# Ordering the experts of a mixture by their row counts on the chip, and moving a list behind the first expert

## The reference

```
logits = xt @ w_router + b_router              # 1024 tokens, 32 experts
top_vals, top_idx = top_k(logits, 4)
gates = softmax(top_vals)
xs = xt[tok]                                   # 4096 rows, sorted by expert
h = ragged_dot(xs, w_gate_up, group_sizes) + b_gate_up[e]
act = min(glu, 7) * sigmoid(1.702 * glu) * (clip(lin, -7, 7) + 1)
y = ragged_dot(act, w_down, group_sizes) + b_down[e]
out = segment_sum(y * gate, tok)
```

## Time and profile before

| | us |
|---|---|
| median of 3 runs | 3243.78 |
| lowest and highest | 3241.05, 3246.48 |
| the profiled execution | 3245.3 |
| its span, first to last instruction | 3243.0 |
| TensorE busy in it | 2861.4 (88%) |
| VectorE, ScalarE, GpSimd busy | 1193.4, 612.3, 196.7 |
| mean granted TensorE clock | 0.944 of full speed |

### The profile page before, as it was taken

One profiled execution on the slowest core, in us unless ns is written; L12 is line 12 of the kernel. 1 busy time (PEld: TensorE's weight loads), 2 busy tenths in 40 slices (PEclk: granted clock), 3 DMA queues, 4 the chain that ended last, 5 costly groups with the idle time before them and its releaser, 6 DMA issues.

```text
span 3243.0 us, 53552 instructions
## 1 busy us (share of the span) xinstructions
PE 2861.4 (88%) x19249; PEld 2455.6 (76%) x19250; DVE 1193.4 (37%) x3107; ACT 612.3 (19%) x1355; POOL 196.7 (6%) x257
## 2 busy tenths in 40 slices
PE   7999899999999996879988889899989998898980
PEld 5444477775477765879988889889989998898980
DVE  1111166663212226324322234323335443343446
ACT  0333233332011111111110111111111111111211
POOL 0000000001000001001000000000001000000100
PEclk9999899999999997989999999899999998999995
DMA  6111311122100006557554567456557875676737
GB/s 246 43 55 45 106 35 44 45 88 80 71 33 0 0 0 247 205 191 257 199 191 157 199 239 292 176 185 226 216 219 283 295 280 195 227 273 228 288 121 265
DMA packets 91043, 530.87 MB, mean 164 GB/s; under 512 B 20528, under 2 KB 42224, under 8 KB 65264
## 3 DMA queue, kind: packets, MB, share of 16 engines
q1 hardware_dynamic: 70992, 490.27, 41.8%
q0 software_dynamic: 18720, 33.60, 2.9%
q10 hardware_dynamic: 1152, 4.19, 0.3%
HBM read 510.14 MB, written 52.46 MB: 173 GB/s over the span
## 4 chain that ended last, share of the span: by engine, by line
PE 83%; issue 8%; DVE 4%; DMA 2%; ACT 2%; DVEq 1%; ACTq 1%; POOL 0%; POOLq 0%; SPq 0%
PE bank L989 48%; PE wide L989 22%; PE bank L982 5%; PE wide L1092 4%; PE bank L1109 3%; DMA ye<-d_y 1%; PE bank L1273 1%; DVE acc L1840 1%; ACT prob L819 1%; ACT st_q L799 1%; DVE mx L1497 1%; DVEq L1799 0%; PE wide L1095 0%; DVE biased L1502 0%; DVE act_t L1805 0%
## 5 line engine op out<-in xcount | busy, mean ns | idle before, releaser
L989 PE MATMUL bank<-xe_t,slot 128*128 128x128 f32 (+2 forms) x8192 | 1089.9, 296 | 187.2 <-issue 187.2
L989 PEld LDWEIGHTS bank<-xe_t,slot 128*128 128x128 f32 x8192 | 1077.2, 197 | 194.8 <-issue 194.3
L989 PE MATMUL wide<-act_t,slot 128*128 128x128 f32 (+2 forms) x4096 | 535.1, 290 | 8.4 <-DVE act_t L1805 7.6
L989 PEld LDWEIGHTS wide<-act_t,slot 128*128 128x128 f32 x4096 | 522.9, 191 | 13.3 <-DVE act_t L1805 13.2
L1793 DVE TENSOR_SCALAR glu<-bank,b_gu 128x256 f32<-128x256 f32 x256 | 123.8, 484 | 1011.3 <-PE bank L989 999.4
L931 ACT ACTIVATE sig<-glu 128x256 f32<-128x256 f32 x256 | 106.7, 417 | 1070.3 <-DVE glu L1793 1016.4
L989 PE MATMUL bank<-w_in,xt 128*128 128x512 f32 (+1 forms) x512 | 216.5, 579 | 3.8 <-DVEq L1426 3.8
L938 ACT ACTIVATE y_t<-wide,b_dn 128x256 f32<-128x256 f32 x256 | 107.3, 470 | 461.1 <-PE wide L989 461.1
L989 PEld LDWEIGHTS bank<-w_in,xt 128*128 128x128 f32 x512 | 96.7, 191 | 111.1 <-issue 110.4
L689 POOL DMA_INDIRECT xg<-d_xn,gidx x66 | 68.2, 1034 | 1727.8 <-DVEq L1708 1717.7
L1805 DVE TENSOR_TENSOR act_t<-lin,sig 128x256 f32<-128x256 f32 x256 | 109.3, 427 | 39.9 <-issue 5.0
(11 more groups left out here) (242 smaller groups left out, 2488.0 us busy)
## 6 DMA issues: line engine op xcount, KB each, us to landing
slot<-in_w_gu SPq DMA_DIRECT2D x128, 2048.0 KB, 7.8
slot<-in_w_dn SPq DMA_DIRECT2D x64, 2048.0 KB, 7.8
ye<-d_y SPq DMA_DIRECT2D x8, 2048.0 KB, 10.4
w_in<-in_w_in SPq DMA_DIRECT2D x1, 6144.0 KB, 30.9
w_mem_k<-in_w_mem_kv SPq DMA_DIRECT2D x1, 4096.0 KB, 15.8
w_mem_v<-in_w_mem_kv SPq DMA_DIRECT2D x1, 4096.0 KB, 25.6
x_sb<-in_x SPq DMA_DIRECT2D x8, 512.0 KB, 3.6
cneg<-d_cneg SPq DMA_DIRECT2D x8, 512.0 KB, 4.9
```

What stands on the lines that cost most here:

```text
L989: m = pe.matmul(dst, l, r_, start=(k == 0), stop=(k == n - 1))
```

## The change

It does four things. It ranks the experts on VectorE by their row count (cut at 256), largest first, equal ones by number, with expert 0 forced to the front; items 0 to 31 then hold the experts and counts in this order. It makes SyncE, ScalarE and VectorE read the expert of every item from the table. It moves the list of further blocks and the gate shares behind VectorE's step 0, which is taken out of the loop. And it moves the small buffers that must now live longer to where the router's weights and logits lay; `place`, for the ranking, takes the old place. TensorE's and GpSimd's code is unchanged.

```diff
--- before.py
+++ after.py
@@ -125,10 +125,22 @@
         sums = keep("sums", [P, 32])
         rstd = keep("rstd", [P, 32])
         CN, XN, RN = 0, 16, 24
+        counts_at = keep.at
         w_r = keep("w_r", [P, KD, E])
         rn_t = keep("rn_t", [P, KD, P])
         lg = keep("lg", [P, NT, E])
+        counts_end = keep.at
         xscale = keep("xscale", [P, NT])
+        cnt = keep("cnt", [P, E])
+        keep.at, keep_at = counts_at, keep.at
+        more = keep("more", [P, 4, E])
+        NQ = S.MORE + 2
+        le = keep("le", [P, NQ, E])
+        le2 = keep("le2", [P, NQ, E])
+        ov = keep("ov", [P, 8, NQ])
+        gate_sum = keep("gate_sum", [P, NT])
+        assert keep.at <= counts_end
+        keep.at = keep_at
         h_res = Region(15, 47)("h_res", [P, NT, D])
         km = Region(47, 55)("km", [P, KD, S.M])
         vm = Region(55, 63)("vm", [P, S.MT, D])
@@ -211,7 +223,6 @@
         val8 = r("val8", [P, NT, 8])
         idx8 = r("idx8", [P, NT, 8], U32)
         idxf = r("idxf", [P, NT, 8])
-        gate_sum = r("gate_sum", [P, NT])
         eq = r("eq", [P, NT, S.TOP, E])
         eqj = r("eqj", [P, NT, S.TOP, E])
         jrow = r("jrow", [P, S.TOP])
@@ -219,12 +230,7 @@
         sel_b = r("sel_b", [P, NT, E], BF16)
         run_b = r("run_b", [P, NT + 1, E], BF16)
         r = Region(191, 207)
-        cnt = r("cnt", [P, E])
-        more = r("more", [P, 4, E])
-        NQ = S.MORE + 2
-        le = r("le", [P, NQ, E])
-        le2 = r("le2", [P, NQ, E])
-        ov = r("ov", [P, 8, NQ])
+        place = r("place", [P, 4, E])
 
         SLOTS = 6
         slots = [Region(95 + 16 * c, 111 + 16 * c)(f"slot{c}", [P, KD, 512]) for c in range(SLOTS)]
@@ -575,14 +581,14 @@
                     sp.wait_ge(e_w[c].free, i)
                     load(slots[c][:, :, :], expert_part(c, e), e_w[c].full)
 
-            with sp.Fori(1, E) as i:
-                refill(i, i)
-
-            def sp_further(i):
+            def sp_item(i):
                 e = sp.value_load(items[0:1, 0, bass.ds(i, 1)], min_val=0, max_val=E - 1)
                 refill(i, e)
 
-            further_blocks(sp, sp_further)
+            with sp.Fori(1, E) as i:
+                sp_item(i)
+
+            further_blocks(sp, sp_item)
             barrier(sp, 7)
 
             load(g_fin[:, :], a["ln_final"].partition_broadcast(P), ld["g_fin"])
@@ -944,13 +950,15 @@
                 ac.drain().then_inc(e_yt, 1)
 
             step(0, 0, None)
+            def expert_at(i):
+                return ac.value_load(items[0:1, 0, bass.ds(i, 1)], min_val=0, max_val=E - 1)
+
             with ac.Fori(1, E) as i:
-                step(i, i, i - 1)
+                step(i, expert_at(i), i - 1)
             rows_back(E - 1)
 
             def ac_further(i):
-                e = ac.value_load(items[0:1, 0, bass.ds(i, 1)], min_val=0, max_val=E - 1)
-                step(i, e, None)
+                step(i, expert_at(i), None)
                 rows_back(i)
 
             further_blocks(ac, ac_further)
@@ -1726,67 +1734,45 @@
             ve.drain()
             hots(0, 0)
 
-            ve.tensor_copy(items[:, 0, 0:E], iota[:, 0:E])
-            ve.tensor_scalar(items[:, 1, 0:E], cnt[:, :], float(CAP), None, ALU.min)
             indices(0)
             ve.sem_inc(e_idx, 1)
             ve.tensor_copy(ixp[:, :], ixs[:, :])
             ve.memset(items[:, 2, 0:E], 1)
-            for b in range(3):
-                ve.tensor_scalar(more[:, b, :], cnt[:, :], float(CAP * (b + 1)), None, ALU.is_gt)
+            pair, pair2 = (v[:, :, :, :].rearrange("p t j e -> p (t j) e") for v in (eq, eqj))
+            size, order, where, picked = (place[:, k, :] for k in range(4))
+            across, down = (lambda v: v.unsqueeze(1).to_broadcast([P, E, E])), \
+                (lambda v: v.unsqueeze(2).to_broadcast([P, E, E]))
+            ve.tensor_scalar(size, cnt[:, :], float(CAP), None, ALU.min)
             ve.drain()
-            ve.tensor_tensor(more[:, 0, :], more[:, 0, :], more[:, 1, :], ALU.add)
+            ve.scalar_tensor_tensor(out=order, in0=size, scalar=-float(E), in1=iota[:, 0:E], op0=ALU.mult, op1=ALU.add)
             ve.drain()
-            ve.tensor_tensor(more[:, 0, :], more[:, 0, :], more[:, 2, :], ALU.add)
-            ve.memset(more[:, 1, :], 1.0)
+            ve.memset(order[:, 0:1], -float(E * (CAP + 1)))
             ve.drain()
-            ve.tensor_tensor_scan(more[:, 2, :], more[:, 1, :], more[:, 0, :], 0.0, ALU.mult, ALU.add)
+            ve.tensor_tensor(pair, across(order), down(order), ALU.is_lt)
             ve.drain()
-            q_row = iota[:, 0:NQ]
-            total = more[:, 2, :].unsqueeze(1).to_broadcast([P, NQ, E])
-            ve.tensor_tensor(le[:, :, :], total, q_row.unsqueeze(2).to_broadcast([P, NQ, E]), ALU.is_le)
+            ve.tensor_reduce(where, pair, AX, ALU.add)
             ve.drain()
-            ve.tensor_tensor(le2[:, :, :], le[:, :, :], more[:, 0:1, :].to_broadcast([P, NQ, E]), ALU.mult)
-            ve.tensor_reduce(ov[:, 0, :], le[:, :, :], AX, ALU.add)
+            ve.tensor_tensor(pair, across(where), down(iota[:, 0:E]), ALU.is_equal)
             ve.drain()
-            ve.tensor_reduce(ov[:, 1, :], le2[:, :, :], AX, ALU.add)
-            ve.tensor_scalar(ov[:, 2, :], ov[:, 0, :], float(E), None, ALU.is_lt)
+            ve.tensor_tensor(pair2, pair, across(iota[:, 0:E]), ALU.mult)
+            ve.tensor_tensor(pair, pair, across(size), ALU.mult)
             ve.drain()
-            ve.tensor_tensor(ov[:, 3, :], q_row, ov[:, 1, :], ALU.subtract)
-            ve.tensor_tensor(le[:, :, :], iota[:, 0:E].unsqueeze(1).to_broadcast([P, NQ, E]),
-                             ov[:, 0, :].unsqueeze(2).to_broadcast([P, NQ, E]), ALU.is_equal)
+            ve.tensor_reduce(picked, pair2, AX, ALU.add)
+            ve.tensor_reduce(where, pair, AX, ALU.add)
             ve.drain()
-            ve.tensor_scalar(ov[:, 3, :], ov[:, 3, :], 1.0, float(CAP), ALU.add, ALU.mult)
-            ve.tensor_tensor(le2[:, :, :], le[:, :, :], cnt[:, :].unsqueeze(1).to_broadcast([P, NQ, E]), ALU.mult)
-            ve.drain()
-            ve.tensor_reduce(ov[:, 4, :], le2[:, :, :], AX, ALU.add)
-            ve.drain()
-            ve.tensor_tensor(ov[:, 4, :], ov[:, 4, :], ov[:, 3, :], ALU.subtract)
-            ve.tensor_scalar(shift[:, E:E + NQ], ov[:, 3, :], 0.0, None, ALU.add)
-            ve.tensor_scalar(ov[:, 5, :], ov[:, 0, :], float(E - 1), None, ALU.min)
-            ve.drain()
-            ve.tensor_scalar(ov[:, 4, :], ov[:, 4, :], 0.0, float(CAP), ALU.max, ALU.min)
-            ve.tensor_copy(items[:, 0, E:E + NQ], ov[:, 5, :])
-            ve.tensor_copy(items[:, 2, E:E + NQ], ov[:, 2, :])
-
-            ve.tensor_scalar(ov[:, 6, :], ov[:, 2, :], -float(8 * T), float(8 * T), ALU.mult, ALU.add)
-            ve.drain()
-            ve.tensor_copy(items[:, 1, E:E + NQ], ov[:, 4, :])
-            ve.tensor_tensor(shift[:, E:E + NQ], shift[:, E:E + NQ], ov[:, 6, :], ALU.add)
-            ve.wait_ge(r_ex, 1)
-            ve.tensor_reduce(gate_sum[:, :], gates[:, :, :], AX, ALU.add)
-            ve.drain()
-            ve.reciprocal(gate_sum[:, :], gate_sum[:, :])
-            ve.drain()
-            ve.tensor_tensor(gates[:, :, :], gates[:, :, :], gate_sum[:, :].unsqueeze(2).to_broadcast([P, NT, S.TOP]),
-                             ALU.mult)
+            ve.tensor_copy(items[:, 0, 0:E], picked)
+            ve.tensor_copy(items[:, 1, 0:E], where)
             x_copies(0)
             barrier(ve, 6)
-            hots(1, 1)
+
+            def expert_at(i):
+                return ve.value_load(items[0:1, 0, bass.ds(i, 1)], min_val=0, max_val=E - 1)
+
+            hots(1, expert_at(1))
 
 
             def step(i, e):
-                nxt = ve.value_load(items[0:1, 0, bass.ds(i + 2, 1)], min_val=0, max_val=E - 1)
+                nxt = expert_at(i + 2)
                 for m in range(KD):
                     b = m % 2
                     ve.wait_ge(e_gu[b].full, e_gu[b].base + 4 * i + m // 2 + 1)
@@ -1816,14 +1802,68 @@
                 hots(i + 2, nxt)
 
             ve.wait_ge(ld["bias"], 32)
-            with ve.Fori(0, E) as i:
-                step(i, i)
-
-            def ve_further(i):
-                e = ve.value_load(items[0:1, 0, bass.ds(i, 1)], min_val=0, max_val=E - 1)
-                step(i, e)
-
-            further_blocks(ve, ve_further)
+            def ve_item(i):
+                step(i, expert_at(i))
+
+            def items_beyond():
+                for b in range(3):
+                    ve.tensor_scalar(more[:, b, :], cnt[:, :], float(CAP * (b + 1)), None, ALU.is_gt)
+                ve.drain()
+                ve.tensor_tensor(more[:, 0, :], more[:, 0, :], more[:, 1, :], ALU.add)
+                ve.drain()
+                ve.tensor_tensor(more[:, 0, :], more[:, 0, :], more[:, 2, :], ALU.add)
+                ve.memset(more[:, 1, :], 1.0)
+                ve.drain()
```

(50 more changed lines are left out.)

## The result

The changed kernel took 3275.14 us (3268.64 to 3279.38), the one before 3244.59 beside it (3241.05 to 3246.48): 1.0094 times, 95% interval 1.0072 to 1.0115, or 23 to 37 us slower. The prediction was 3269, slower, in a range of 3253 to 3279. The profiled execution took 3271.7 us against 3245.3, its span 3269.4 against 3243.0: +26.4.

A forecast was written before the change was run, and what follows sets the result against it. TensorE's waits for code around wide laps were taken to bound. Step terms sum to 1868.9 against 1845.1 us, +23.8; ranking adds 1.3; 3243.8 + 25.1 = 3269 us, range 3253 to 3279.

The forecast's parts named there:

- What bounds: Expert stage: TensorE idles 187.2 us ahead of the gate and up product, waiting for code in each wide lap.
- a lap of nine: Instruction queue: a lap of the 160 body moves nine packets and refetches all; a lap of the 128 body moves none.
- step 0 to the next: Start of the first expert step to the next: body 47.73, gap 10.50 and extra jump 4.2, together 62.4 us.
- the 208s: Four 208 column steps: bodies 293.6, three gaps of 16.2 and one of 12.0, together 354.2 us.
- the 160s: Nine 160 column steps: bodies 523.8, eight gaps of 15.35 and one of 11.2, together 657.8 us.
- the 128s up to the last step: 128 column steps before the last step's start: first 49.04 and its 0.5, then sixteen of 46.56, together 794.5 us.
- Rival 1: The second jump between 208s is free, three gaps are 12.0: -12.6 us, 3256.5; chance 0.08.
- The 4.2: Extra jump to the 208's own code, priced by the 128 to 208 gap less the short one: 4.2 us.
- Ranking: VectorE before the first copy of expert 0's rows: 9.9 us of ranking replaces 8.6 us of list and shares, +1.3 us.
- The list: Further blocks and gate shares, 8.6 us on VectorE, hide behind step 0 in its 24.16 us wait: cost nothing.
- Rival 2: Equal widths in a row keep their code; eleven gaps fall to 0.5 us: about 3080, faster by 5%; chance 0.07.
- Rivals 3 and 4: Third: moved list's cover fails, +8.6, 3278, chance 0.07. Fourth: gaps shrink, order worth nothing, within 6 us, chance 0.03.

The follow-up runs named there:

- the hint: The changed kernel with a branch prefetch hint for the loop's closing branch at the head of each TensorE lap: 3257.11 us, 1.0049 of before.

## Why the prediction was right

**What bounds.** The reading of the idle time as waits for code in wide laps held. The idle time moved with the place of a body in the code (one execution), went when each loop had one body, and didn't follow the width or the number of changes. Two sizes worked out from the same reading missed, the returns with two bodies (by 65 us) and the hint (18 us of 90).

One part of the reading is not borne out. The prediction calls a 160 lap "a lap of nine" blocks and the 128 lap shorter. But both run about the same code (x424 to x432 matmuls against x416), and a lap needs about four blocks, as the loops with one body show. So the nine are more than the lap's own code. Why a lap through the second or the third place of four bodies fetches again, and one through the first or the last doesn't, no run here shows.

**The sum by its terms,** forecast and measured in the profile: step 0 to the next 62.4 and 62.9; the 208s 354.2 and 359.1; the 160s 657.8 and 656.6; the 128s up to the last step 794.5 and 794.8; together 1868.9 and 1873.4, against 1845.1 before. The unseen case, 208 behind 208, was the one to choose, and the upper bound was the right end: 16.2 forecast, 17.3 measured on average, the rest of the term being bodies of 73.9 instead of 73.4. Rival 1 (12.0 us) falls.

There was luck in that choice. Rival 1 had more for it than the prediction says. The chain of the kernel before has two gaps from a 160 to a 208:

```profile
1706.57 15.21 issue
...
2075.54 15.34 issue
```

They are no longer than the two from a 160 to a 160, 15.49 and 15.21, so behind a 160 the jump on to the 208's own code cost nothing more. By these rows a 208 behind a 208 would have been put near the 12.04 from a 208 to a 160. The 4.2 that the prediction added was seen only behind a 128, and behind a 208 it came to 5.5 (17.3 less 11.8); why it showed there and not behind a 160 stays open.

**Ranking** 1.3 forecast, 1.1 measured; the dearer price of the reductions did not apply. The prediction put the whole 8.6 us of the old list on the path. Only the last 2.3 were, as the run with the moved list alone shows; the sum didn't suffer, since the ranking is longer than the 8.6 and what is added at the end counts in full. **The list** was hidden.

**The total.** 25.1 us were forecast. The profile has 28.3 between the first step and the last and 1.1 ahead of them, less 3.0 after the start of the last step, which makes the span's 26.4. That last stretch took 138.2 us before and 135.3 after; over the ten kernels of this document it took between 135.3 and 138.2, one profiled execution each, so the 3 us are no more than what it varies by; nothing ties them to the change. The median moved by 30.6. Its interval of 23 to 37 holds the 25.1 as well as the 26.4.

**Rival 2** (equal widths in a row keep their code) is false for the 160s and 208s in this code, but it is true in the shorter loop of two bodies, in loops with one body each, and for the 160s once they stand first. It named the right condition, that a lap must stay loaded. **Rivals 3 and 4** did not occur.

The Trainium skill ("Runtime: NRT & Kernel Launch", Instruction fetch mechanics) gives TensorE 128 KiB of instruction memory in blocks of 16 KiB. The trace agrees on the blocks: the 142 packets of the stage moved 2.33 MB, 16.4 KB each. On the 128 KiB it says less. Laps of about four blocks stay loaded, but laps through the second and third place of four bodies, with about as many instructions, don't, so the size alone doesn't decide. The section's sentence on a window of two blocks doesn't fit the 128 laps, which need about four and fetched none in sixteen laps of the changed kernel.

## What to carry to other kernels

Where the chain of waits shows "issue" ahead of TensorE's next product, look at the branch's own duration and at the instruction queue's packets per lap before reordering data. Packets show which laps refetch; only the gap and the branch show what it costs. A loop over several unrolled bodies can pay on every lap whose code doesn't stay loaded, whether or not the same branch is taken again. Ordering the work by size was worth something only together with code that uses it: alone it cost 0.9%, with one loop for each size it gained 6.2%. A cheaper variant may be to put the rare bodies, not the frequent ones, in the middle of the code, since the first and the last place both kept their laps; that rests on one execution, and on the grouped order alone.

## What had not been expected

The last place in the chain of bodies kept its laps as the first does: 128 to 128 took 46.5 us there. Only the way into it cost something, some 8 us of idle time around the start of each of the first two 128s. Turning the bodies round brought the grouped order to 3126.9 us in its one execution, 3.6% under before. And the number of code blocks fetched in the stage was nearly the same before and after, 143 and 142 packets, while the idle time ahead of the product differed by 33 us. With two bodies it was the other way about: 54 packets more cost 11 us.
